# Strassen products in the gated and deep projections of a 6-layer float32 transformer kernel

## Time and profile before

| | |
|---|---|
| runs | 2638.62, 2643.52, 2645.17 us; median 2643.52 |
| the profiled execution | 2645.21 us, span 2643.4 us |
| busy, of the span | TensorE 96%, weight loads 77%, VectorE 42%, ScalarE 19%, POOL 4% |
| mean granted TensorE clock | 0.971 of full speed |
| DMA | 452.98 MB, mean 171 GB/s |

### The profile page before, as it was taken

How to read it: one execution, slowest core, us unless ns; L and a number is a source line. 1 busy time by engine, 2 the same in 40 slices (tenths; PEclk the granted TensorE clock), 3 DMA queues, 4 the chain that set the end, 5 groups by cost and what they waited for, 6 DMA issues and landing times.

```text
span 2643.4 us, 32942 instructions
## 1 busy us (share of the span) xinstructions
PE 2527.6 (96%) x12508; PEld 2033.8 (77%) x12508; DVE 1119.8 (42%) x2464; ACT 497.1 (19%) x1237; POOL 110.8 (4%) x212
## 2 busy tenths in 40 slices
PE   7899999998899999999999899999999999999997
PEld 4465888754558888589889588898788887789887
DVE  4844123256541123333554445643844653423321
ACT  2222100024321001112211232102222101103210
POOL 0000000000000000000101001110001110000000
PEclk9889999996899999999999999999999999999999
DMA  5124467530125566435777247684227774434441
GB/s 227 66 96 156 138 207 244 200 130 1 47 92 199 183 232 214 168 125 177 253 257 282 77 151 255 248 294 159 104 96 264 254 279 174 176 126 144 151 152 56
DMA packets 122329, 452.98 MB, mean 171 GB/s; under 512 B 13776, under 2 KB 13904, under 8 KB 121680
## 3 DMA queue, kind: packets, MB, share of 16 engines
q1 hardware_dynamic: 92880, 338.24, 35.8%
q0 software_dynamic: 29312, 112.80, 12.3%
HBM read 449.93 MB, written 1.05 MB: 171 GB/s over the span
## 4 chain that ended last, share of the span: by engine, by line
PE 89%; DVE 6%; ACT 2%; issue 1%; DMA 1%; POOL 0%; SPq 0%; DVEq 0%; ACTq 0%
PE pair L462 82%; PE bank L462 6%; DVE att_s L1330 1%; DVE arena L1325 1%; DVE h L1215 1%; ACT arena L970 1%; DVE rstd L1212 1%; DMA arena<-gmws_dram 1%; ACT arena L982 1%; PE bank L601 0%; DVE arena L1746 0%; DVE arena L1742 0%; DMA cst<-consts_dram 0%; ACT arena L961 0%; PE bank L628 0%
## 5 line engine op out<-in xcount | busy, mean ns | idle before, releaser
L462 PE MATMUL pair<-h,ring 128*128 128x256 f32 (+1 forms) x5344 | 1122.6, 373 | 19.7 <-DVE x L1240 6.8
L462 PEld LDWEIGHTS pair<-h,ring 128*128 128x128 f32 x5344 | 989.9, 192 | 148.9 <-DVE x L1240 7.2
L462 PE MATMUL pair<-arena,ring 128*128 128x256 f32 (+1 forms) x3312 | 638.2, 355 | 3.7 <-issue 2.1
L462 PEld LDWEIGHTS pair<-arena,ring 128*128 128x128 f32 x3312 | 569.7, 192 | 72.7 <-issue 3.5
L462 PE MATMUL pair<-ring,h 128*128 128x512 f32 (+1 forms) x768 | 324.3, 580 | 3.0 <-DVE h L1215 3.0
L462 PEld LDWEIGHTS pair<-ring,h 128*128 128x128 f32 x768 | 142.0, 190 | 169.5 <-issue 163.2
L1408 DVE CUSTOM_DVE_ANT_0 adat<-adat,crow,cols 128x1024 f32<-128x1024 f32 x192 | 241.6, 1277 | 6.5 <-DMA adat<-adaw_dram 6.5
L1386 DVE SCALAR_TENSOR_TENSOR arena<-pair,cols,arena 128x255 f32<-128x255 f32 x176 | 84.9, 482 | 279.5 <-ACT arena L1018 279.5
L1018 ACT ACTIVATE arena<-pair,cols 128x256 f32<-128x256 f32 x176 | 99.2, 563 | 463.4 <-PE pair L462 463.4
L940 ACT ACTIVATE h<-x 128x256 f32<-128x256 f32 x84 | 35.0, 417 | 692.5 <-DVE x L1241 364.0
L419 POOL DMA_DIRECT2D adat<-adaw_dram x192 | 101.3, 528 | 1315.4 <-DVE mod L1408 1289.5
(11 more groups left out here) (193 smaller groups left out, 1306.3 us busy)
## 6 DMA issues: line engine op xcount, KB each, us to landing
ring<-stream_dram SPq DMA_DIRECT2D x638, 512.0 KB, 4.0
adat<-adaw_dram POOLq DMA_DIRECT2D x192, 512.0 KB, 4.6
arena<-gmrows_dram POOLq DMA_DIRECT2D x2, 2560.0 KB, 11.1
arena<-cmpw_dram POOLq DMA_DIRECT2D x1, 2112.0 KB, 8.3
x<-x_in_dram SPq DMA_DIRECT2D x2, 512.0 KB, 4.7
arena<-mem_in_dram SPq DMA_DIRECT2D x1, 1024.0 KB, 12.9
arena<-gmws_dram POOLq DMA_DIRECT2D x2, 512.0 KB, 13.1
out_dram<-h POOLq DMA_DIRECT2D x2, 512.0 KB, 3.8
```

Of the source, the lines that this page charges most:

```text
L462: return nc.tensor.matmul(out, lhsT, rhs, start=start, stop=stop)
```

## The change

For 21 pairs of output tiles in up0 and up1 (gate tile t and value tile 22 + t, t = 1 to 21) and 3 pairs in each of the six deep projections, the product of two output tiles with two token halves and K inputs is computed by Strassen's scheme in Winograd's form: seven products of K/2 weight tiles with 128 tokens in place of eight. (Odd and even input tiles are the two halves of the depth.) The remaining tiles, two in each projection, stay as head or tail halves. cup0 to cup3 are not changed.

- TensorE: `seven`, `product`. Each pair uses two banks, 5 and 6 or 7 and 3 in turn, with a slot of 128 columns for each product; weights of four products are sums in SBUF.
- VectorE forms the four weight sums of a pair (`weight_sum`): for a gated pair each 4 tiles wide (512 columns), two pairs ahead (`up_weights`); for a deep pair each 11 tiles wide (1408 columns), into a single buffer (`down_weights`), so each is written only when TensorE has read that of the pair before. It forms four sums of the inputs (`moving_sums`), and combines the seven results (`combined`) with one of them copied out of PSUM by ScalarE (`first_copy`).
- SiLU, gating and residual now read combined tiles in SBUF.
- Slabs are released once a pair, at its first product; a deep pair after the first releases its own at its fourth product.
- `ada_tile`: in conv after six of seven tiles in place of two of three (38 for 30 in a layer), in cdown 10 for 18.

The diff, cut to its core (lines deep inside `build` stand eight spaces to the left):

```diff
-    return [Linear("up" + tag, "F", DK, 2 * FT, "act+dve"), Linear("down" + tag, "F", FT, DK, "dve")]
+    return [Linear("up" + tag, "S", DK, 2 * FT, "dve"), Linear("down" + tag, "S", FT, DK, "dve")]
...
+        n = {"F": lin.N, "T": 2 * -(-lin.N // 4), "S": 0}[lin.kind]
+        places = [[(group + i) % 2] for i in range(n)]
+        if lin.kind == "S":
+    grows = lin.K < lin.N
+    lin.head = [0, FT] if grows else []
+    lin.pairs = [(t, FT + t) for t in range(1, FT)] if grows else [(n, n + 1) for n in range(0, lin.N - TAIL, 2)]
+    lin.tail = [] if grows else list(range(lin.N - TAIL, lin.N))
+    lin.ktiles = [(j, min(KBLOCK, lin.K // 2 - j)) for j in range(0, lin.K // 2, KBLOCK)]
...
+    for _ in lin.pairs:
+        places.append(PAIRS[pairs % 2])
+        engines.append("dve")
...
+PAIRS = ([5, 6], [7, 3])
...
+    if lin.kind == "S":
+        out = [(k, n) for n in lin.head for k in range(lin.K)]
+        for a, b in lin.pairs:
+    out += [(2 * j + e, n) for n in (a, b) for e in range(2) for j in range(lin.K // 2)]
+        return out + [(k, n) for n in lin.tail for k in range(lin.K)]
...
+    def seven(name, moving, sums, ready, sums_done, norm=None):
+        lin = PLAN[name]
...
+        g += len(lin.head)
+        half_k = lin.K // 2
+        for p in range(len(lin.pairs)):
+            q = lin.pair0 + p
+            own = [upW[:, q % 2, m] for m in range(4)] if lin.head else downW[name != "down0"]
+            bank_free(g)
+            one, two = (banks[b] for b in USED[g])
+            def product(bank, slot, stationary, move, check=None, free=None):
+                for j in range(half_k):
+                    if check is not None and p == 0:
+                        check(j)
+                    ins = mm(bank[:, slot * P:slot * P + P], stationary(j), move(j), j == 0, j == half_k - 1)
+                    if j == 0 and free is not None:
+                        release(ins, True, free)
+                return ins
+            def summed(m):
+                if lin.head:
+                    pe.wait_ge(sem("up_summed"), q + 1)
+                else:
+                    pe.wait_ge(sem("down_summed"), 4 * q + (m + 1 if p == 0 else 4))
+            product(one, 0, lambda j: tile(t + j), lambda j: moving(2 * j)[:, HALVES[0]],
+                    lambda j: ready(None, 2 * j, 0), t)
+            product(one, 1, lambda j: tile(t + half_k + j), lambda j: moving(2 * j + 1)[:, HALVES[0]],
+                    lambda j: ready(None, 2 * j + 1, 0))
+            if p == 0:
+                pe.wait_ge(sem("moving_summed"), sums_done)
+            product(two, 3, lambda j: tile(t + 3 * half_k + j), lambda j: sums[:, 3, j, :])
+            summed(0)
+            ins = product(two, 0, lambda j: own[0][:, j, :], lambda j: sums[:, 0, j, :], None,
+                          t + 2 * lin.K if not lin.head and p else None)
+            if not lin.head:
+                ins.then_inc(sem("down_read"), 1)
+                summed(1)
+            ins = product(two, 1, lambda j: own[2][:, j, :], lambda j: sums[:, 2, j, :])
+            if not lin.head:
+                ins.then_inc(sem("down_read"), 1)
+                summed(2)
+            ins = product(one, 2, lambda j: own[1][:, j, :], lambda j: sums[:, 1, j, :])
+            if not lin.head:
+                ins.then_inc(sem("down_read"), 1)
+                summed(3)
+            ins = product(two, 2, lambda j: own[3][:, j, :], lambda j: moving(2 * j + 1)[:, HALVES[1]])
+            ins.then_inc(sem("mm_done"), 1)
...
+    def down(name, norm):
+        def ready(at, k, half):
+            if name in ("down0", "down1"):
+                if k:
+                    pe.wait_ge(sem("hid_up"), (FT - 1) * int(name[-1]) + k)
+                else:
+                    pe.wait_ge(sem("freed_dve"), FREER[PLAN["up" + name[-1]].g0 + 1][1])
+            else:
+                pe.wait_ge(sem("hid_done"), FT * int(name[-1]) + k + 1)
+        seven(name, lambda k: hid[:, k, :], downT, ready, MOVING_SUMS[name] + len(PLAN[name].ktiles), norm)
...
     def ffn(i, norm):
-        linear(f"up{i}", lambda k: h[:, k, :], h_ready(f"ffn{i}"), head=HEAD)
+        ready = h_ready(f"ffn{i}")
+        seven(f"up{i}", lambda k: h[:, k, :], upT[i],
+              lambda at, k, half: at is not None and ready(at, k, half),
+              MOVING_SUMS[f"up{i}"] + 1)
+        down(f"down{i}", norm)
...
+    def first_copy(g, e):
+        act.wait_ge(sem("mm_done"), g + 1)
+        nc.scalar.copy(e[:, 7, :], banks[USED[g][0]][:, 0:P]).then_inc(sem("first_copied"), 1)
...
+        act.wait_ge(sem("mm_done"), lin.g0 + 1)
+        nc.scalar.activation(hid[:, 0, :], banks[USED[lin.g0][0]][:, 0:TOK], ACT.Silu
+                             ).then_inc(sem("freed_act"), 1)
+        for t in range(1, FT):
+            first_copy(lin.g0 + 1 + t, ebuf[:, t % 2])
+            act.wait_ge(sem("freed_dve"), FREER[lin.g0 + 1 + t][1])
+            nc.scalar.activation(hid[:, t, :], ebuf[:, t % 2, 0:2, :].rearrange("p a q -> p (a q)"), ACT.Silu
+                                 ).then_inc(sem("gated"), 1)
...
+        if before is not None:
+            before()
+        for p in range(len(lin.pairs) if lin.kind == "S" else 0):
+            for r in range(4):
+                if p + 1 < len(lin.pairs):
+                    down_weights(name)
+                if between is not None and r < 3:
+                    between(3 * p + r)
+            e = ebuf[:, p % 2]
+            link(combined(lin.g0 + p, e))
+            if gate is None:
+                xs = x[:, 2 * p:2 * p + 2, :].rearrange("p a t -> p (a t)")
+                V.tensor_tensor(xs, e[:, 0:4, :].rearrange("p s q -> p (s q)"), xs, ALU.add
+                                ).then_inc(sem("freed_dve"), 1)
+            else:
+                for a in range(2):
+                    n = 2 * p + a
+                    ins = V.scalar_tensor_tensor(x[:, n, :], e[:, 2 * a:2 * a + 2, :].rearrange("p s q -> p (s q)"),
+                                                 gate[:, n:n + 1], x[:, n, :], ALU.mult, ALU.add)
+                ins.then_inc(sem("freed_dve"), 1)
+            for k in range(max(1, 2 * p - 2), 2 * p):
+                add_squares(k, slice(0, TOK), k + 1)
...
+    def weight_sum(base, w, own, m):
+        slabs_seen[0] = max(slabs_seen[0], base // SLAB)
+        while slabs_seen[0] <= (base + 4 * w - 1) // SLAB:
+            d = slabs_seen[0]
+            dve.wait_ge(sem(f"slab_in{d % RING}"), 16 * (d // RING + 1))
+            slabs_seen[0] += 1
...
+        for a, b in zip(cuts, cuts[1:]):
+            s = [o[:, a:b, :] for o in own]
+            if m == 0:
+                ins = V.tensor_tensor(s[0], part(2, a, b), part(3, a, b), ALU.add)
+            elif m == 1:
+                ins = V.tensor_tensor(s[1], s[0], part(0, a, b), ALU.subtract)
+            elif m == 2:
+                ins = V.tensor_tensor(s[2], part(0, a, b), part(2, a, b), ALU.subtract)
+            else:
+                ins = V.tensor_tensor(s[3], part(1, a, b), s[1], ALU.subtract)
+        return ins
+    def up_weights(i):
+        lin = PLAN[f"up{i}"]
+        q = up_pairs[0]
+        up_pairs[0] += 1
+        base = lin.tile0 + lin.K * len(lin.head) + 2 * lin.K * (q - lin.pair0)
+        if q >= 2:
+            dve.wait_ge(sem("mm_done"), PLAN[f"up{(q - 2) // (FT - 1)}"].g0 + 3 + (q - 2) % (FT - 1))
+        own = [upW[:, q % 2, m] for m in range(4)]
+        weight_sum(base, DK // 2, own, 2)
+        link(weight_sum(base, DK // 2, own, 0))
+        link(weight_sum(base, DK // 2, own, 1))
+        weight_sum(base, DK // 2, own, 3).then_inc(sem("up_summed"), 1)
+    def down_weights(name):
+        lin = PLAN[name]
+        q, r = divmod(down_sums[0], 4)
+        down_sums[0] += 1
+        if q >= lin.pair0 + len(lin.pairs):
+            raise ValueError(name)
+        if q:
+            dve.wait_ge(sem("down_read" if r < 3 else "mm_done"), 3 * (q - 1) + r + 1 if r < 3 else DOWN_GROUP[q - 1])
+        if r >= 2:
+            dve.wait_ge(sem("down_summed"), 4 * q + r + 1 - 2 + (r == 3))
+        base = lin.tile0 + 2 * lin.K * (q - lin.pair0)
+        weight_sum(base, FT // 2, downW[name != "down0"], (0, 2, 1, 3)[r]).then_inc(sem("down_summed"), 1)
+    def moving_sums(src, dst, j, w):
+        b = src[:, 2 * j:2 * (j + w), :].rearrange("p (j a) t -> p j a t", a=2)
+        b11, b12, b21, b22 = (b[:, :, a, HALVES[i]] for a in range(2) for i in range(TT))
+        t1, t2, t3, t4 = (dst[:, i, j:j + w, :] for i in range(4))
+        V.tensor_tensor(t3, b22, b12, ALU.subtract)
+        link(V.tensor_tensor(t1, b12, b11, ALU.subtract))
+        link(V.tensor_tensor(t2, b22, t1, ALU.subtract))
+        V.tensor_tensor(t4, b21, t2, ALU.subtract).then_inc(sem("moving_summed"), 1)
+    def combined(g, e):
+        dve.wait_ge(sem("first_copied"), FIRST[g])
+        one, two = (banks[b].rearrange("p (s q) -> p s q", q=P) for b in USED[g])
```

(43 more changed lines are left out.)

176 lines of the change are left out of this document (128 added, 48 removed).

## The result

The changed kernel takes 2622.53 us (median of four runs, 2614.72 to 2622.83) against 2644.35 for the kernel before on the same chip: ratio 0.991, with its 95% interval [0.9882, 0.9939]. That is 21.8 us less where 48.9 less were forecast. The profiled execution took 2622.7 us, its span 2620.9 (2643.4 before).

What follows compares the result with a forecast made beforehand. TensorE, busy 96% of the span, was taken as the bound. Products save 63.0 us; waits of 2, 1.4, 3.8, 1.8, 1.6 and 3.5 leave 48.9, so 2645.2 becomes 2596 us; eight-in-ten range 2583 to 2630.

Steps and rivals of the forecast that it cites:

- the first pair's weights ahead of the memory output projection: Before the memory output projection's residual: 2.7 us of VectorE sums, bank wanted after 3.5, so no cost.
- the last slab of the deep pairs: Second deep pair: slab there 11.4 to 13.1 us in, nothing lost; worst case 0.8 us in down0 and down1.
- The price of a half product: TensorE product with 128 tokens: 0.2232 us, two instructions of 0.1116 us, 0.515 of a whole product.
- B: Rival: a half product on TensorE costs 0.2346 us, gain 19.7 us, total 2625 us; chance 0.09.
- D: Rival: a narrow product costs much more than half; at 0.60 of a whole one, 2690 us; chance 0.02.
- C: Rival: TensorE products start with a gap, an exposed weight load each, 81 us, total 2677 us; chance 0.09.
- The stops in the gated projections: Where hidden-input sums and a modulation tile share a round, TensorE waits 0.5 us, four times, 2 us.
- From gated to deep: Start of the deep projection after up0 and up1: TensorE waits 1.9 us, twice, 3.8 us.
- Conv: Conv projections: 0.3 us twice in three layers, 1.8; into the deep projection 0.4 us in four, 1.6.
- Layer 2: Conv projection waiting on tiles loaded after the gated MLP's rows: 3.5 us more wait, 6.3 us idle.
- Start of up0: `mem_source(1)` stands ahead of the sums of h on VectorE, so TensorE waits 1.4 us.
- A: Rival: VectorE or slabs late, 0.3 us per gated pair and 2 us in five deep projections, 2619 us; chance 0.14.

Runs made afterwards that it cites:

- second and third joined versions: Changed kernel with memv freed at attention, gated MLP rows last, `mem_source` after first sums, second-pair tiles before sums: 2590.79 us; same with slabs of 4: 2598.86 us.

## Why the prediction was right and wrong

The direction and the price of the products held, the waits didn't: 2622.5 lies in the range, but 26.5 us above the forecast, and the gain is 21.8 of the 48.9 us. Two steps failed, and between them they are 20 us: the first pair's weights ahead of the memory output projection, priced at nothing (13.8 us measured), and the last slab of the deep pairs, of which nothing was taken as lost (6.5 us of waits).

**Right.** The price of a half product: 56 instructions in 6.25 us and 154 in 17.19, 0.1116 us each. So B falls, with D: the ratio is 0.515 in operation too. C falls: in three deep pairs of cdown3, 51.58 us, TensorE had no idle time, and in 125 us of a gated projection 0.50. The stops in the gated projections: 0.25 us of idle and a piece of 6.49 in place of 6.25, 0.49 each, forecast 0.5. From gated to deep: 1.17 us of idle ahead of the third product and 0.27 in the piece behind it (12.55 us for 110 instructions), 1.4 where 1.9 were forecast. Conv: 0.14 for 0.3 at the two spots (7.04 us for 6.90 of work), 0.47 for 0.4 to the deep projection. Layer 2: a stop of 5.50 us, forecast 6.3. With the slower products behind it, which the forecast left out, it cost 8.2 us, 3.4 more than in the kernel before, forecast 3.5: the two errors cancel. That the stage as a whole is only 0.7 us off is luck too, for its mixer was 1.5 us faster in this execution and hid the 1.5 us wait for the slab. cup3 and cdown3: 5.4 us less, forecast 5.2. Start of up0: waits of 0.48 and 0.69, forecast 1.4. There 20 instructions also took 4.63 us that took 3.52 in the kernel before, at a lower clock. That is neither the change nor the stop ahead of them: they took 4.64 us with memv freed, 4.64 in the kernel before with its rows last, and 2.50 in the changed kernel with small slabs. The range's lower end is mis-stated: with the start (1.4) and layer 2 (3.5) real it is 2645.2 - 63.0 + 4.9 = 2587, not 2583.

**Wrong, first:** "The first pair's weights are made ahead of the memory output projection's residual, 2.7 us, where the bank is wanted after 3.5: nothing." The durations were right, and freeing memv shows that they cost nothing. What failed is that I took the weights to be in the ring. I counted VectorE's time at this place and not the ring's 88 tiles against what is alive: 32 + 32 + 16 + 16. The first pair's 16, behind the head's 16 in the stream, are now wanted a stage earlier, and I priced the earlier step without asking when its inputs can be asked for. Cost: 13.8 us in two places, 3.77 and 3.71 of it stops, 3.2 and 3.1 slower products around them. The prediction had about 1 us each as the price if the cover were gone.

**Wrong, second:** in the deep pairs "it is there 11.4 to 13.1 us into the pair" and "I take nothing as lost". It was there after 13.8, 14.4, 16.1, 16.4 and 15.8 us. The bound came from 2560 + 512 KB in 13.1 us, counted from the start of the pair as if six slabs were all that was under way. For slabs alone that holds: in cdown3 the slab came after 12.6 us. What the step left out are the modulation tiles' own loads. I counted the tiles as VectorE's work, 1.3 us each, and not as 512 KB each on DMA engines that the slabs already fill. Four such loads went with 16.1 us and, in the run with the tiles first, seven with 18.6; that the number of loads is the cause rests on these three places, and no run took the loads alone away. Then the sum of sums and tiles was as I had it. The waits are 6.5 us in five projections; the worst case in the text was 0.8 in two. By the prediction's own sign, a deep pair over 17.5 us, this step is wrong: the third pair of cdown0 takes 19.0.

**Of the rivals** A was the nearest, 2619 us, and its second half ("the slabs come late") is what happened in the deep projections, at 0.7 to 1.8 us where it had 2. Its first half, 0.3 us in each gated pair, didn't happen. Its total was right for another reason, the memory stage, which no rival had.

**Left over** are 4.0 us in code that the change doesn't touch. The stretch from 488 to 740 us, the same in all kernels, took between 246 and 255 us, and the first memory output projection, with nothing changed ahead of it, began between 246.1 and 249.7, so 4.0 us is within the scatter. The stages of layers 0 and 1 miss about 1 us more than their waits: a stop costs about 0.25 us beyond the idle time that the view shows. With two stops, 0.28 us idle together, the 704 instructions of cup0 took 150.34 us that took 149.53 in cup3 without one; 110 behind a stop took 12.55 us for 12.28 of work, and 88 took 10.06 where the next 88 took 9.83.

## What to carry to other kernels

Where an edit brings a step forward, count what it needs in the ring or pool at its new place, tile by tile, with the moment at which each older tenant is released; the duration of the step is the smaller question. A tile that waits for the last transfer of a burst takes the burst's time, not the median of a transfer, and the loads of other queues count in the burst; so put behind it only what depends on it, and ahead of it what doesn't. Moving work from one pair to another only moved the wait; moving it into VectorE's idle time in the same pair took the wait away.

## What was not expected of the hardware

A stop of 3.8 us in TensorE cost 7.0. The granted clock was 0.74 in the 11.7 us behind it, where the same products without the stop ran at 1.00. Over the kernels here that kept the stop the last 48 instructions took 10.5 to 12.0 us, so the size of this loss varies from run to run. In the 15 us after that the clock is 0.77 with the stop and without it, so only the projection's own part is the stop's.

The length of a stop alone doesn't say what follows. At the third deep pair 88 instructions took 10.06 us behind waits of 1.88 and 2.48 us (the second and third joined versions), and 11.69 us at a granted clock of 0.85 behind 1.96 us (memv freed with small slabs) and 2.37 us (rows last).

The time from issue to landing of a 512 KB slab was 4.0 us by the median of the kernel before and up to 12.0 where eleven were asked for in a row beside the modulation tiles' loads; beside none it was at most 8.5. With slabs of half the size the first weight sum of the third pair still waited 8.68 us in down0.
